# Norms of the late layers by halves, spectra folded, and the last opening modulation load as TensorE weights

## The reference, cut to what matters

```
m = silu(c) @ w_mod[i] + b_mod[i]          # 9 modulation vectors per layer and stream
def modulated_norm(x, g, shift, scale):     # "pre" norm
    return rms_norm(x, g) * (1 + scale) + shift
def half_step_ffn(x, ...):
    h = modulated_norm(x, g_pre, shift, scale)
    y = (silu(h @ w_gate) * (h @ w_up)) @ w_down
    return x + 0.5 * gate * rms_norm(y, g_post)   # "post" norm
# layer 0: ffn, neighbourhood attention + short conv, ffn
# layer 1: ffn, Hyena: y = irfft(rfft(u) * rfft(k)) with filters k made by a small MLP, ffn
```

## Time and profile before

| | |
|---|---|
| median of 3 runs | 1323.24 us (1322.91 to 1327.0) |
| profiled execution, its own time | 1323.29 us |
| its span, first to last instruction | 1321.6 us |
| PE busy | 1289.4 us, 98% |
| DVE busy | 981.8 us, 74% |
| ACT busy | 636.4 us, 48% |
| mean DMA rate | 209 GB/s |

### The profile page before, as it was taken

The page is one execution under the profiler, slowest core; times in us unless marked ns, Lnnn a source line. Parts: engine busy times, 40 slices in busy tenths (PEclk is TensorE's granted clock), DMA queues, the critical chain, the costliest instruction groups (busy, mean ns, idle before and its releaser), DMA issues.

```text
span 1321.6 us, 21410 instructions
## 1 busy us (share of the span) xinstructions
PE 1289.4 (98%) x7762; PEld 1114.7 (84%) x7762; DVE 981.8 (74%) x1444; ACT 636.4 (48%) x973; POOL 120.2 (9%) x211
## 2 busy tenths in 40 slices
PE   6899999999999999999999999999999999999997
PEld 4678777887778998689998889999998988999996
DVE  5788777788787885758886778888748786865554
ACT  6633333233376665755444456444446435544443
POOL 3000010111100522011110000111000000000000
PEclk9999999999999999999999999999999999999999
DMA  9555667777755753269886555998654535656652
GB/s 357 210 175 177 204 204 239 258 240 254 243 171 177 220 152 104 80 181 348 300 300 195 163 166 198 311 357 287 205 178 144 160 118 200 228 180 184 188 188 99
DMA packets 76472, 275.65 MB, mean 209 GB/s; under 512 B 9274, under 2 KB 9829, under 8 KB 75760
## 3 DMA queue, kind: packets, MB, share of 16 engines
q1 hardware_dynamic: 52128, 187.00, 43.4%
q0 software_dynamic: 24272, 87.65, 19.7%
HBM read 273.57 MB, written 1.05 MB: 208 GB/s over the span
## 4 chain that ended last, share of the span: by engine, by line
PE 84%; DVE 8%; ACT 3%; DMA 2%; issue 2%; DVEq 0%; ACTq 0%; SPq 0%; POOLq 0%
PE gu L1700 16%; PE gu L1702 16%; PE gu L1701 16%; PE acc L1765 8%; PE acc L1767 8%; PE acc L1766 8%; DVE wlo_r L1024 2%; DMA wlo<-in_wstream_dram 2%; PE acc L1754 2%; ACT whi L625 1%; PE acc L2029 1%; PE acc L2027 1%; PE acc L2028 1%; PE gu L1809 1%; PE job_p L2194 1%
## 5 line engine op out<-in xcount | busy, mean ns | idle before, releaser
L1700 PE MATMUL gu<-h_hi,whi 128*128 128x256 f32 (+1 forms) x1688 | 517.6, 307 | 2.9 <-DVE h_lo L1153 1.3
L1701 PE MATMUL gu<-h_lo,whi 128*128 128x256 f32 (+1 forms) x1688 | 515.2, 305 | 0.0
L1702 PE MATMUL gu<-h_hi,wlo_r 128*128 128x256 f32 (+1 forms) x1688 | 514.8, 305 | 0.0
L1024 DVE TENSOR_TENSOR wlo_r<-wlo,whi 128x1024 fp32r<-128x1024 f32 x350 | 422.1, 1223 | 92.2 <-ACT whi L625 90.2
L625 ACT ACTIVATE whi<-wlo 128x1024 fp32r<-128x1024 f32 x350 | 360.9, 1049 | 86.7 <-DMA wlo<-in_wstream_dram 86.1
L1700 PEld LDWEIGHTS gu<-h_hi,whi 128*128 128x128 f32 x1688 | 318.6, 189 | 26.2 <-issue 3.2
L1701 PEld LDWEIGHTS gu<-h_lo,whi 128*128 128x128 f32 x1688 | 318.6, 189 | 19.2 <-issue 0.7
L1702 PEld LDWEIGHTS gu<-h_hi,wlo_r 128*128 128x128 f32 x1688 | 319.2, 189 | 15.5
L1041 DVE SCALAR_TENSOR_TENSOR part<-wm,cvec,part 128x512 f32<-128x512 f32 x266 | 199.4, 750 | 6.7
L1765 PE MATMUL acc<-whi,act_hi 128*128 128x512 f32 x440 | 175.8, 399 | 1.6 <-DVE act_lo L1241 1.1
L1767 PE MATMUL acc<-wlo_r,act_hi 128*128 128x512 f32 x440 | 174.1, 396 | 0.0
(11 more groups left out here) (349 smaller groups left out, 1214.1 us busy)
## 6 DMA issues: line engine op xcount, KB each, us to landing
wlo<-in_wstream_dram SPq DMA_DIRECT2D x350, 512.0 KB, 3.6
wm<-in_wmod_dram POOLq DMA_DIRECT2D x132, 512.0 KB, 5.9
area<-in_wmod_dram POOLq DMA_DIRECT2D x11, 512.0 KB, 19.8
z<-in_gate_rows_dram POOLq DMA_DIRECT2D x6, 512.0 KB, 9.6
gate_keep<-in_gate_rows_dram POOLq DMA_DIRECT2D x5, 512.0 KB, 8.9
area<-in_rpb_dram POOLq DMA_DIRECT2D x32, 64.0 KB, 3.6
x_lat<-in_x_in_dram SPq DMA_DIRECT2D x1, 1024.0 KB, 7.9
area<-in_ctx_in_dram SPq DMA_DIRECT2D x1, 1024.0 KB, 8.8
```

Source lines behind the costliest of these rows:

```text
L1024: nc.vector.tensor_tensor(wlo[:, u.base % RING, :], raw[:, u.base % RING, :], whi[:, u.base % RING, :].bitcast(F32), ALU.subtract).then_in ...
L1700: nc.tensor.matmul(out_, w_hi, x_hi, start=start, stop=False, skip_group_check=True)
L1701: nc.tensor.matmul(out_, w_hi, x_lo, start=False, stop=False, skip_group_check=True)
L1702: return nc.tensor.matmul(out_, w_lo, x_hi, start=False, stop=stop, skip_group_check=True)
```

## The change

1. **Post norms by halves.** In norms 6, 8, 10, 12 and 14 ACT squares the first 512 columns of y when PE has finished that half (a new semaphore, `y_half`), turns that sum into `mean_half` (a one-column instruction), squares the second 512, and takes the root of the sum with `mean_half` as its bias. DVE's `times_gate` likewise runs as two halves of 512. ACT's first weight split now stands between tile 0 and tile 1, not behind both.
2. **Pre norms 7, 9, 11, 13** join norms 3 and 5 (SCALED): DVE scales x by rstd over 1024 columns into `spare`, and PE transposes that (8 transposes for each tile). DVE has no split between the two tiles; the two splits stand in `late_los`, one between lo5 and lo6, one behind lo7.
3. **ACT's columns** follow LATE_STEPS: hi2, hi0, hi1, z2, hi3, z3, hi6, hi4, z6, hi5, hi7, z7; hi from PSUM comes before its z.
4. **Spectra folded.** Each `spectrum(i)` is one matmul instead of two; all four of a seam stand ahead of `norm_columns`. DVE rebuilds the full spectra by a sum and a difference over 128 x 1024 (`unfold`): two in feed-forward 2, turn 9, two at steps 4 and 5 of the Hyena projection.
5. **The opening.** Load 3 (chunks 12 to 15) is no longer split into hi and lo. PE takes each 128 x 128 block of it as weights and moves the two columns of `cvec` past it, 32 matmuls in all, so that the results are columns at once; `row(3)` and `ahead_columns(3)` are gone. PE's order around it changes, 16 matmuls of the identity (EARLY) stand at PE's very beginning, behind the arrival of `ident`, and POOL issues the next modulation load only when chunk 15 has landed. Units 2 to 5 no longer wait for chunks 14 and 15 to be read.

```diff
-CHUNK_SLOT = [2, 3, 4, 5, 2, 3, 4, 5, 2, 3, None, 4, 5, None, 4, 5]
+SPLIT_CHUNKS = 12
+CHUNK_SLOT = [2, 3, 4, 5, 2, 3, 4, 5, 2, 3, None, 4]
+SCALED = (3, 5, 7, 9, 11, 13)
+LATE_STEPS = (("hi", 2), ("hi", 0), ("hi", 1), ("z", 2), ("hi", 3), ("z", 3),
+              ("hi", 6), ("hi", 4), ("z", 6), ("hi", 5), ("hi", 7), ("z", 7))
...
+            pool.wait_ge(ahead_landed[AHEAD_CHUNKS - 1], 16)
             load_job(AHEAD, ahead_lo, lambda part_: 4)
-            pool.wait_ge(ahead_lo, AHEAD_CHUNKS)
+            pool.wait_ge(ahead_used, AHEAD_CHUNKS)
...
+            def square_y(q, t):
+                i, k = 2 * q + t, 2 * (NTH[q] - 2) + t
+                a.wait_ge(y_half, 2 * (NTH[q] - 1) + t + 1)
+                nc.scalar.activation(square_out, y_tile(t)[:, 0:512], ACT.Square,
+                                     accum_out=ssum_half[:, k:k + 1]).then_inc(half_done, 1)
+                a.wait_ge(half_done, k + 1)
+                nc.scalar.activation(mean_half[:, k:k + 1], ssum_half[:, k:k + 1], ACT.Identity, bias=eps[:, 0:1],
+                                     scale=1.0 / D).then_inc(mean_done, 1)
+                if t == 0:
+                    a.wait_ge(y_done, NTH[q] + 1)
+                else:
+                    a.wait_ge(pe_done, Y_END[NTH[q]])
+                nc.scalar.activation(square_out, y_tile(t)[:, 512:D], ACT.Square,
+                                     accum_out=ssum[:, i:i + 1]).then_inc(ss_done, 1)
+                a.wait_ge(mean_done, k + 1)
+                a.wait_ge(ss_done, i + 1)
+                nc.scalar.activation(root[:, i:i + 1], ssum[:, i:i + 1], ACT.Sqrt, bias=mean_half[:, k:k + 1],
+                                     scale=1.0 / D).then_inc(root_done, 1)
...
             def norms(q, held):
-                square(q, 0)
-                square(q, 1)
+                square_y(q, 0)
                 for u in held[:1]:
                     split(Unit(u))
+                square_y(q, 1)
                 if q + 1 < len(NORMS):
                     square(q + 1, 0)
                     square(q + 1, 1)
                     for u in held[1:]:
                         split(Unit(u))
-                    h_his(q + 1)
+                    late_his(q + 1)
...
+                h_lo_of(q, 4)
+                h_lo_of(q, 5)
+                split(Unit(held[0]))
+                h_lo_of(q, 6)
+                h_lo_of(q, 7)
+                split(Unit(held[1]))
...
-            def times_gate(q, t, cols=slice(0, D)):
+            def times_gate(q, t):
...
+                for half, cols in enumerate((slice(0, 512), slice(512, D))):
+                    if half == 0:
+                        v.wait_ge(half_done, 2 * (NTH[q] - 2) + t + 1)
+                    else:
+                        v.wait_ge(ss_done, 2 * q + t + 1)
+                    nc.vector.tensor_tensor(z_tok[:, t, cols], y_tile(t)[:, cols], gate_tile[layer, block_, stream][:, cols],
+                                            ALU.mult).then_inc(z_done, 1)
...
+                    if n >= SPLIT_CHUNKS:
+                        if kt % 2 == 0:
+                            pe.wait_ge(ahead_landed[n], 16)
+                        for i in range(4):
+                            ins = nc.tensor.matmul(rows_[:, 2 * i:2 * i + 2], flat_chunk(n)[:, cols][:, i * P:(i + 1) * P],
+                                                   cvec[:, kt, :], start=(kt == 0 and i == 0), stop=(kt == KT - 1),
+                                                   skip_group_check=True)
...
+            pe.wait_ge(ident_landed, 16)
+            for _ in range(EARLY):
+                nc.tensor.matmul(mean_p[:, 0:P], ident[:, :], ident[:, :], start=True, stop=True)
             pe.wait_ge(c_lo, 1)
             ahead(0, (0, 1))
             norm_columns(0, 0)
             norm_columns(0, 1)
             ahead(0, range(2, KT))
-            ahead(1)
+            ahead(1, range(0, 4))
+            norm_columns(1, 0)
+            ahead(1, range(4, KT))
             pe.wait_ge(picked, 1)
             ahead_columns(0)
-            norm_columns(1, 0)
+            norm_columns(1, 1)
             ahead_columns(1)
-            norm_columns(1, 1)
             ahead(2)
+            ahead(3, range(0, 2))
             ahead_columns(2)
-            ahead(3, (0, 1))
+            ahead(3, range(2, KT))
             first_tiles(LAT, range(0, 4))
-            ahead(3, range(2, KT))
-            first_tiles(CTX, range(0, 2))
-            ahead_columns(3)
-            first_tiles(CTX, range(2, 4))
+            first_tiles(CTX, range(0, 4))
             first_tiles(LAT, range(4, KT))
             first_tiles(CTX, range(4, KT))
...
+UNFOLD_AT, UNFOLD_HY = [(9, 0), (9, 4)], (4, 5)
```

More of the change, by code:

```diff
@@ L385, in last_chunk @@
         def last_chunk(slot):
-            return max(n for n in range(AHEAD_CHUNKS) if CHUNK_SLOT[n] == slot)
+            return max(n for n in range(SPLIT_CHUNKS) if CHUNK_SLOT[n] == slot)
         def ahead_bank(l):
@@ new lines, in late_his @@
+            def late_his(q):
+                p = NTH[q]
+                _, layer, stream, _, shift, _ = NORMS[q]
+                for what, kt in LATE_STEPS:
+                    col = mod_column(layer, shift, stream, kt)
+                    if kt not in LATE_Z:
+                        a.wait_ge(zt_done, scaled(q, kt))
+                        nc.scalar.activation(late_hi[:, kt, :], z[:, kt, :], ACT.Copy).then_inc(hh_done, 1)
+                    elif what == "hi":
+                        a.wait_ge(coef_done, coef_count(q, kt))
+                        a.wait_ge(mod_ready, shift_count(q, kt))
+                        a.wait_ge(hp_done, 4 * p + kt // 2 + 1)
+                        nc.scalar.activation(late_hi[:, kt, :], columns_of(q, kt), ACT.Identity, bias=mod[:, col:col + 1],
+                                             scale=coef[:, p, kt:kt + 1]).then_inc(hh_done, 1)
+                    else:
+                        nc.scalar.activation(z[:, kt, :], columns_of(q, kt), ACT.Identity, bias=mod[:, col:col + 1],
+                                             scale=coef[:, p, kt:kt + 1]).then_inc(late_z, 1)
@@ L823, in _ @@
             row(2)
-            for n in (13, 14, 15):
-                chunk_hi(n)
             h_his(1, HI_ORDER[:4])
-            row(3)
             split_hi(2, 2)
@@ L1172, in h_los @@
                 scale_columns(q, 5)
-                for kt in range(4, KT):
-                    h_lo_of(q, kt)
+                h_lo_of(q, 4)
[4 more added lines that the diff above has]
+                split(Unit(held[1]))
             def first_los(half):
@@ L1216, in add_scaled, with norms @@
                                                op0=ALU.mult, op1=ALU.add).then_inc(x_upd, 1)
-            def post(q):
+            def norms(q, held):
                 for t in range(2):
@@ L1223, in post @@
                     add_scaled(q, t)
-            def norms(q, held):
-                post(q)
                 spread(q + 1, 0)
-                split(Unit(held[0]))
                 spread(q + 1, 1)
-                h_los(q + 1)
-                split(Unit(held[1]))
+                late_los(q + 1, held)
             def gate_up(n, s, dst):
@@ L1376, in _ @@
             ahead_out(1)
+            chunk_lo(11)
             first_coef(0, 0)
@@ L1687, in _ @@
             for t in range(2):
-                halves = [slice(0, 512), slice(512, D)]
-                for cols in halves:
-                    times_gate(14, t, cols)
+                times_gate(14, t)
                 reciprocal(14, t)
-                for half, cols in enumerate(halves):
-                    add_scaled(14, t, cols, 2 * 6 + 2 * t + half)
+                for cols in (slice(0, 512), slice(512, D)):
+                    add_scaled(14, t, cols)
         @block.tensor
@@ L2086, in last_projected @@
                             pe.wait_ge(m_ready, ready + j)
-                        ins = token_product(t, False, j == 1, m_hi[:, kt, :], m_lo[:, kt, :], u.plus(j).base % RING)
+                        for half in range(2):
+                            ins = token_product(t, False, j == 1, m_hi[:, kt, :], m_lo[:, kt, :], u.plus(j).base % RING, (half,))
+                            if j == 1 and half == 0:
+                                ins.then_inc(y_half, 1)
                         if t == 1:
@@ L2129, in spectrum @@
             def spectrum(i):
-                half, what, w = SPECTRUM[i]
+                half, what, th = SPECTRUM[i]
                 cols = slice(half * 512, half * 512 + 512)
-                for th in range(2):
-                    base, x_ = (0, p_f) if what == "re" else (2, m_f)
-                    ins = nc.tensor.matmul(spectrum_bank(i), dft[:, base + th, w * P:(w + 1) * P], x_[:, th, cols],
-                                           start=(th == 0), stop=(th == 1))
-                ins.then_inc(fp, 1)
+                base, x_ = (0, p_f) if what == "re" else (2, m_f)
```

(4 more changed lines are left out.)

115 lines of the change are left out of this document (68 added, 47 removed).

## The result

The changed kernel took 1327.49 us (median of 20 runs, 1324.96 to 1330.46) against 1323.24 us of the kernel before in the same comparison; the ratio is 1.0029, 95% interval 1.002 to 1.0038. The prediction was 1317.8 us with a range up to 1321.5: wrong in size and in sign. The profiled execution took 1329.85 us (span 1328.2), 6.6 us more in span than the profile of before.

A forecast was written before the change was run, and what follows sets the result against it. TensorE, busy 1289.4 of 1321.6 us, was taken as the bound, leaving the opening and seams to gain. Terms 2.5 + 0.95 + 0.95 + 1.1 - 0.65 + 0.85 - 0.2 = 5.5 us gave 1317.8, range 1313.5 to 1321.5.

The forecast's parts named there:

- The opening: Program start to the end of the first tiles: 3.8 us gained, less 1.3 for a clock fall, so 2.5 gained.
- the weight-bound records lose little: Load 3's 48 records: 0.12 us each, 5.9 us in all, hardly slower when the clock falls.
- the opening gives nothing: Rival: at 0.21 us a record load 3 ends 4.3 us later, time 1322; chance 0.07.
- Norms 7, 9, 13: Seams between y and the next units: gains of 0.95, 1.1 and 0.95 us from halves and scaled transposes.
- the wait for h_lo: First units of the seams: the split between lo5 and lo6 delays lo6, so TensorE waits 0.6 us.
- The late norms give nothing: Rival: each late seam costs 0.7 us more than summed, 3.0 us gone, time 1320.8; chance 0.12.
- Norm 11 and Hyena: Norm 11's seam loses 0.65 us; two unfolds in the Hyena projection lose 0.2 us.
- the clock falls in the late seams too: Rival: idle TensorE lets the clock fall at late norms, 1.3 us each, two or more 1320.4 to 1322; chance 0.14.
- The order of lo7 behind the split: Norm 11: lo7 ends the seam, second unit at 1006.4 instead of 1005.77, a loss of 0.65 us.
- The end: Behind the last y: tile 0's first gate half done ahead and four adds without a gap, 0.85 us gained.
- the unfolds: VectorE rebuilding spectra, about 1.2 us each: two cost nothing, two in the Hyena projection lose 0.2 us.
- The slower rival: Rival: load 3's weight loads don't overlap with moving columns, 0.43 us a record, time 1332; chance 0.04.

The follow-up runs named there:

- no_early: The changed kernel without the 16 identity matmuls at the program's start (`EARLY = 0`); 1327.82 us in one run.
- late_only: Kernel before plus the late norms alone (items 1 to 3), with the opening and spectra of before; 1322.2 us, ratio 0.9987.
- late_split_first: late_only with VectorE's weight split of the first held unit put back ahead of the lo blocks; 1322.14 us, ratio 0.9977.
- full_open: The changed kernel plus 11 needless matmuls of 128 weight columns and 512 moving columns in the opening; 1331.51 us, executed once.
- steady: late_split_first plus 28 identity matmuls where TensorE waits in the opening, 7 of them behind an added wait; 1321.03 us, ratio 0.9984.
- late_fold: The changed kernel with the opening of before, keeping late norms and folded spectra; 1324.12 us, ratio 1.0001.
- opening_only: Kernel before with item 5 of the change (the opening) and nothing else; 1326.56 us against 1324.66, ratio 1.0011.
- warm_open: The changed kernel plus 28 identity matmuls of 128 x 128 in the opening, 12 in a wait and 2 behind each 8 records; 1332.5 us, executed once.

## Why the prediction was wrong

- **The opening (predicted -2.5, came +4.87): the step that failed.** I took the 48 records at 0.12 us and wrote that "the weight-bound records lose little" by a fall of the clock, for which I allowed 1.3 us. At the full clock the price was right (0.10 to 0.115 us), but at 1.2 GHz it is 0.214, and the fall lasted 17.1 us, not 3.4. It added 10.3 - 48 x 0.10 = 5.5 us to the records; 26 tiles at 0.213 instead of 0.118 cost 2.5 more. Without these 8 us tile 2 would start near 57.2, and my estimate (tiles done at 55.7, so tile 2 near 56.3) is not far from that; but no run shows this opening with the clock up and nothing added. Term by term: the 48 records took 4.4 us more than the 5.9 of the sum, the tiles 14.1 us where I had 11.3 + 1.3, and the records began 1.9 us later than I had them (40.38, not 38.5). Part of the last is not the long fall: chunk 10, which I took to land as before (28.02), came at 28.93, and the row's copy at 38.25, not 37.4. Why it landed later stays open; it did in all six kernels with this opening and its warm-up (28.9 to 29.5), and not in no_early (27.97). The rival "the opening gives nothing" had the price, 0.21 us, but not the tiles behind the records.
- **Reading the row before.** The trace of before may have had the case in small: two-column matmuls in a window, and the clock down in the next. (It is not certain that they were the cause: late_only, with the same code and the same matmuls, has no fall there.) I carried the length of that one fall over to a stretch in which nothing ended it. In before it ended after three microseconds of tiles; in after nothing but two-column records ran until 50.6 us, and the clock came back 5.6 us into the tiles.
- **Norms 7, 9, 13 (-0.95, -1.1, -0.95; came -0.74, -0.91, -0.40).** Mechanism and nearly the size, with the wait for h_lo of 0.46 to 0.53 us where I had 0.6. At norm 13 VectorE came to its column blocks later as well, and the units took 6.82 us (6.46 at norm 7). late_split_first shows that the wait at norms 7 and 13 was not needed. But I ended the working at the next unit, and in FFN 1 and 2 the gain was gone some 27 us (FFN 1) and 62 us (FFN 2) later, in a wait that goes back to the weight transfers: "The late norms give nothing", for another reason than the one I gave. How much of the +1.04 and +1.12 is this and how much is chance stays open: with the late norms y to y over both blocks took 410.8 to 412.3 us in ten of eleven kernels without an added delay (full_open: 414.5), and 411.3 and 412.5 in the two without them. The medians speak a little better of the late norms: without the fold and with the opening of before, late_only, late_split_first and steady lie 2.1 to 2.2 us below before (intervals from 0.9961 to 1.0 in all). Of this the profiles show the 0.9 us at the end; the rest may be less time at the low clock in the opening (mean clock 0.9979 in late_only and 0.9972 in late_split_first, 0.9963 in before beside them), and the code of the opening is the same in all three. So it stays open.
- **Norm 11 and Hyena (+0.65 and +0.2; came +1.41 and +1.31).** The order of lo7 behind the split was sized rightly: late_only, with no fall of the clock, lost 0.79. The rest is the clock, low from 1005.2 and again from 1012.0; "the clock falls in the late seams too" had a chance of 0.14. It fell at norm 11 in after and not at 7, 9 or 13, and at norms 9 and 11 in late_fold; without the fold at neither in any run. TensorE's own queue of spectra, which I had called the bound, had also kept its clock up.
- **The end (-0.85; came -0.86)** and the unfolds (0.2; 0.25 by late_fold against late_only) were right.
- **The slower rival** had an overlap of weights and columns failing at 0.43 us a record. That isn't what happened, yet the same sign came from a doubling of 0.10. By its own terms this rival makes "slower" from about 0.32 us a record on (0.12 + 9.4/48), not from 0.36.

**The medians.** The profile's 6.6 us are 4.2 in the medians, because the profiled execution of after (1329.85) was 2.4 us slower than its median, while that of before (1323.29) was at its own. Over 29 runs of before, a microsecond more at the low clock (worked out from each run's mean granted clock) goes with 0.42 us more time, correlation 0.91. The mean clock was 0.9962 in before, so 10 us low, of which the profile has 4.4 behind the last y; 0.9921 in opening_only, 21 us; 0.9902 in after, 26 us. By that slope the clock costs opening_only 4.6 us and after 6.7. They lost 1.9 and 4.2. So some 2.5 us of the opening's gain may be real under the loss. This is argued from the slope, not shown, and the slope is rough: it is 0.35 within opening_only and 0.20 within after, and one run of before had a mean clock of 0.945, some 146 us low, and took 1328.55 us, only 5.3 us over its median.

The Trainium skill (TensorE: Matmul & The Clock Gate, section "What's actually happening") says that the clock is set by how busy the array has been. Taken for the profile's busy share, the runs disagree: 100% busy from 36 to 59 us in warm_open with the clock down from 45.8, and 100% busy in full_open with it up. The same page (section "LDWEIGHTS (loading the stationary operand)") gives a weight load as its columns over 1.2, so 107 ns for 128 columns, with no word on the clock; at 2.4 GHz the records come near it (0.10 to 0.115 us), at 1.2 GHz they take 0.214, and the measurement decides. Part 4 ("PE-mode transpose") says that the full level does not engage for transposes. In late_only 8 transposes pass in 1.09 us at PEclk 1.00, so they do run at the full level once it is there; whether they help to hold it no run shows, for in late_fold the clock fell over them, behind 2.02 us of idle time.

## What to carry to other kernels

Where wide moving operands are replaced by loads of 128 x 128 weights with two columns moved past them, don't price it by a count of instructions at the full clock alone: here the clock fell, and the dense work behind it paid too. Work that seems needless on a queue, spectra done in two halves here, may be what holds the clock over a seam. A seam's gain may last only up to the next wait that a transfer sets, so follow the timeline through the block behind it before booking it. The version worth keeping here is the opening and the spectra of before with the late norms and the split put first: 0.9977 of the time before, and 0.9984 for the same with the matmuls of steady, a small gain whose source is only in part known.

## What the runs showed of the hardware that was not expected

- TensorE can be busy for 100% of 14 us and be at 1.2 GHz for nearly all of it (warm_open, 45.3 to 59.4 us); with eleven matmuls of 128 weight columns by 512 moving columns between the same records it stayed at 2.4 GHz for the whole opening (full_open).
- A float32 record of 128 x 128 weights and two moving columns takes 0.10 us at 2.4 GHz (full_open) and 0.214 at 1.2 GHz (after).
- The opening of before started tile 2 at 57.9 to 63.2 us in the profiles of seven kernels (and at 59.2 with the matmuls of steady), with 0 to 10 us at the low clock. Single profiles of this kernel differ by more than most of its edits are worth.
- The trace's record of the granted clock begins late, at 16.7 us in before and at 8.5 in after, and a view shows 1.00 ahead of it; yet in before records with 128 moving columns pass there at 0.21 us each (from 12.5 us on), the pace of the low level. The mean clock of a run doesn't count that time.
